# Memory's keys and values laid in other places, products on other banks, and the delta rule's late steps reordered

## What is computed

```python
h = rmsnorm(x, g_mix)
dq, dk, dv, dz, db, da, cq, ckv, kix, wix = split(h @ w_in)
dq, dk, dv = silu(causal_depthwise_conv([dq, dk, dv], conv_w))
g = -exp(a_log) * softplus(da + dt_bias)            # the gates: log decay per token and head
...
decay = exp(where(incl, g_cum[:, None] - g_cum[None, :], -inf))
a_mat = where(strict, beta * (k @ k.T) * decay, 0) + eye
sol = triangular_solve(a_mat, [v * beta, k * beta * exp(g_cum)])
for chunk in 4 chunks of 64 tokens:                 # gated delta rule, 4 heads
    v_new = u - w @ state; o = q_dec @ state + qk @ v_new; state = state * last + k_dec.T @ v_new
o_dn = rmsnorm(o) * silu(dz)
o_dsa = sparse_attention(cq, ckv, kix, wix)         # 8 heads, top 64 of 256 keys
x = x + concat(o_dn, o_dsa) @ w_out
kvx = rmsnorm(mem, g_mem) @ w_xkv                   # memory's keys and values, for cross attention behind this
```

## Time and profile before

| | us |
|---|---|
| median of 3 runs (lowest, highest) | 977.46 (975.92, 977.53) |
| the profiled execution | 976.31 |
| its span, first to last instruction | 974.5 |

### The profile page before, as it was taken

How to read it: one execution, slowest core, us unless ns; L and a number is a source line. 1 busy time by engine, 2 the same in 40 slices (tenths; PEclk the granted TensorE clock), 3 DMA queues, 4 the chain that set the end, 5 groups by cost and what they waited for, 6 DMA issues and landing times.

```text
span 974.5 us, 15544 instructions
## 1 busy us (share of the span) xinstructions
PE 950.0 (97%) x6212; PEld 848.5 (87%) x6212; DVE 679.7 (70%) x1247; ACT 530.4 (54%) x1011; POOL 125.6 (13%) x147
## 2 busy tenths in 40 slices
PE   8999999999999999999999799999899999999997
PEld 8999888999999988888988788988698898888885
DVE  5888767777478676666667659776665577676765
ACT  6876666765456643434455585664444354434443
POOL 1211111211032000000001115930100000000001
PEclk9999999999999999999999899999999999999999
DMA  9543334234377556565547534211353446656541
GB/s 317 186 140 131 130 105 155 94 124 132 129 252 239 173 181 216 173 215 171 194 152 262 164 108 133 105 44 44 132 172 130 151 138 207 201 170 199 171 168 43
DMA packets 116151, 154.71 MB, mean 159 GB/s; under 512 B 2760, under 2 KB 98256, under 8 KB 115824
## 3 DMA queue, kind: packets, MB, share of 16 engines
q1 hardware_dynamic: 113376, 142.91, 44.2%
q0 software_dynamic: 2240, 10.42, 3.1%
q10 hardware_dynamic: 464, 0.40, 0.2%
HBM read 150.56 MB, written 3.16 MB: 158 GB/s over the span
## 4 chain that ended last, share of the span: by engine, by line
PE 88%; DVE 6%; ACT 4%; issue 1%; DMA 1%; POOL 0%; POOLq 0%; DVEq 0%; SPq 0%; ACTq 0%
PE ps L827 13%; PE ps L803 9%; PE ps L805 8%; PE ps L804 8%; PE ps L828 7%; PE ps L1114 6%; PE ps L846 4%; PE ps L848 4%; PE ps L847 4%; PE ps L1087 4%; PE ps L1088 3%; PE ps L1089 3%; PE ps L789 3%; PE ps L816 2%; PE ps L818 2%; PE ps L817 2%
## 5 line engine op out<-in xcount | busy, mean ns | idle before, releaser
L1347 DVE TENSOR_TENSOR wlo<-raw,whi 128x1024 fp32r<-128x1024 f32 (+1 forms) x268 | 327.0, 1238 | 165.7 <-ACT whi L1958 165.4
L1958 ACT ACTIVATE whi<-raw 128x1024 fp32r<-128x1024 f32 (+1 forms) x268 | 274.4, 1051 | 138.3 <-PE ps L828 53.9
L827 PE MATMUL ps<-R1b,whi 128*128 128x512 f32 x576 | 201.8, 393 | 0.3 <-DVE wlo L1347 0.3
L803 PE MATMUL ps<-R1b,whi 128*128 128x256 f32 (+1 forms) x592 | 173.1, 292 | 5.5 <-DVE F L1635 3.0
L805 PE MATMUL ps<-R1b,wlo 128*128 128x256 f32 (+1 forms) x592 | 168.0, 284 | 0.0
L804 PE MATMUL ps<-R1b,whi 128*128 128x256 f32 (+1 forms) x592 | 167.8, 283 | 0.0
L828 PE MATMUL ps<-R1b,wlo 128*128 128x256 f32 x576 | 161.4, 280 | 0.0
L827 PEld LDWEIGHTS ps<-R1b,whi 128*128 128x128 f32 x576 | 108.1, 188 | 25.0 <-issue 0.8
L803 PEld LDWEIGHTS ps<-R1b,whi 128*128 128x128 f32 x592 | 112.0, 189 | 16.0 <-issue 8.6
L805 PEld LDWEIGHTS ps<-R1b,wlo 128*128 128x128 f32 x592 | 112.1, 189 | 0.0
L804 PEld LDWEIGHTS ps<-R1b,whi 128*128 128x128 f32 x592 | 111.8, 189 | 0.2
(11 more groups left out here) (279 smaller groups left out, 1786.6 us busy)
## 6 DMA issues: line engine op xcount, KB each, us to landing
raw<-in_w_in SPq DMA_DIRECT2D x34, 1024.0 KB, 5.1
raw<-in_w_ffn_in SPq DMA_DIRECT2D x22, 1024.0 KB, 5.1
raw<-in_w_ffn_out SPq DMA_DIRECT2D x11, 1024.0 KB, 5.5
raw<-in_w_gate SPq DMA_DIRECT2D x11, 1024.0 KB, 5.3
raw<-in_w_up SPq DMA_DIRECT2D x11, 1024.0 KB, 5.3
raw<-in_w_down SPq DMA_DIRECT2D x11, 1024.0 KB, 5.6
raw<-in_w_out SPq DMA_DIRECT2D x8, 1024.0 KB, 5.1
raw<-in_w_xkv SPq DMA_DIRECT2D x8, 1024.0 KB, 5.5
```

What stands on the lines that cost most here:

```text
L803: e.matmul(o, hi[:, kt, c], R[0][:, kt, 0:n], start=kt == 0, stop=False)
L827: e.matmul(B[:, :].rearrange("p (a n) -> p a n", a=2), hi[:, kt, c], R[2][:, :, kt, 0:256], start=kt == 0, stop=False)
L1347: e.tensor_tensor(half_of(wlo[i % HL], i, k), half_of(raw[i % RAW], i, k), f32(half_of(whi[i % HL], i, k)), SUB).then_inc(lo_split(i, (i, k)))
L1958: return e.activation(o, i, f, **kw)
```

## The change

Five groups of edits, which leave the arithmetic as it is:

- `tail` and the last values of the memory take banks of "four" and no longer of "big". `conv` 4 then finds banks 0 and 1 free since the transposes ahead of `tail`, and `conv` 8 takes bank 0 behind `conv` 6. In turn the memory's last values hold banks 5 and 6 from step 582 of the plan to 599: the sixteen `index` products, which before went round banks 7, 2, 4, 5, 3 and 6, go round 2, 3, 4 and 7, and `index` 0's fifth takes the bank of its first, `ssq` that of `index` 2's first, `kk` that of `index` 3's last.
- Keys lie in SC columns 1024 to 3071, the first values in 3072 to 4095, the last values in F, in Z's place. DT has its columns for itself; what waits for the store now is Xi and KD (`xi0`, `kn`) and, for the last values, Z (`zg`).
- `kvout` 0 moves from step 0 to 6, `kvout` 1 from ahead of `taps` 8 to behind it.
- `cums0`, `decay0`, `cums1` and `decay1` move a product later: `cums0` from behind `conv` 5 to behind `conv` 6, `cums1` and `decay1` (on ACT a table load, three small and eight large exponentials) from ahead of the split of unit 82 and `conv` 7 to behind them.
- At the end `rn_z` 0 and the split of unit 90's second half stand ahead of `chunk` 3, `rn_b` 0 ahead of `o1` 1, and `rn_z` 1 ahead of head 7's division.

```diff
-MIX = [(0, -1, ("kvout", 0)), (12, -1, ("kvout", 1))]
+MIX = [(6, 1, ("kvout", 0)), (13, 1, ("kvout", 1))]
...
-    (4, -1, "gates0", 0), (4, 1, "gates1", 0), (5, -1, "gates2", 0), (5, 1, "cums0", 0), (6, -1, "decay0", 0),
-    (7, -1, "cums1", 0), (7, -1, "decay1", 0), (10, -1, "ssq", 1), (10, 1, "scale", 0), (11, -1, "kk", 0), (11, -1, "inv", 0),
+    (4, -1, "gates0", 0), (4, 1, "gates1", 0), (5, -1, "gates2", 0), (6, 1, "cums0", 0), (7, -1, "decay0", 0),
+    (7, 1, "cums1", 0), (7, 1, "decay1", 0), (10, -1, "ssq", 1), (10, 1, "scale", 0), (11, -1, "kk", 0), (11, -1, "inv", 0),
...
-    (29, 1, "rn_a", 0), (31, 1, "rn_z", 0), (32, -1, "rn_a", 1), (32, 1, "rn_b", 0), (33, 1, "rn_z", 1), (34, 1, "rn_b", 1))]
+    (29, 1, "rn_a", 0), (32, -1, "rn_a", 1), (34, 1, "rn_b", 1))]
...
-MIX += [(31, 1, ("delta", "o1", 1))]
+MIX += [(30, 1, ("delta", "rn_z", 0)), (30, 1, ("ahead",)), (31, 1, ("delta", "rn_b", 0)),
+        (31, 1, ("delta", "o1", 1)), (32, 1, ("delta", "rn_z", 1))]
...
-                    two("mem", (1, u), part, i, ("four", "big")[u], R3a, normed("nm"), lambda t: (mem_act, (1, u, t)))
+                    two("mem", (1, u), part, i, "four", R3a, normed("nm"), lambda t: (mem_act, (1, u, t)))
...
-                two("tail", u, part, i, "big", R1, normed("nx2"), lambda t: (tail_dve, t))
+                two("tail", u, part, i, "four", R1, normed("nx2"), lambda t: (tail_dve, t))
...
                 if name == "decay0":
-                    d.wait_ge(kx_out, 0)
```

More of the change, by code:

```diff
@@ L225, in ahead @@
     def ahead(n=2 * HL, taken=0):
-        step("ahead", len(halves) + n, len(halves) + taken)
+        step("ahead", len(halves) + (n or 2 * HL), len(halves) + taken)
     def take(i, j):
@@ L327, in spread @@
                 if (at, side) == (k, 1):
-                    step(*token)
+                    ahead(0) if token == ("ahead",) else step(*token)
         for work, _ in works:
@@ L632, in program @@
         xsm = [F[:, 6144:7168], F[:, 7168:8192]]
+        keys, values_ = SC[:, 1024:3072].rearrange("p (b n) -> p b n", b=8), (SC[:, 3072:4096], F[:, 6180:7204])
         KX = SC[:, 0:2048].rearrange("p (b n) -> p b n", b=8)
@@ L2101, in mem @@
                         for t in range(2):
-                            act(VX[:, t, 512 * u:512 * u + 512], ps("mem", (1, u), t)[:, :]).then_inc(mem_act((1, u, t)))
+                            act(values_[u][:, 512 * t:512 * t + 512], ps("mem", (1, u), t)[:, :]).then_inc(mem_act((1, u, t)))
                     else:
-                        act(KX[:, 2 * u:2 * u + 2, :], ps("mem", (0, u))[:, :].rearrange("p (b n) -> p b n", b=2)).then_inc(
+                        act(keys[:, 2 * u:2 * u + 2, :], ps("mem", (0, u))[:, :].rearrange("p (b n) -> p b n", b=2)).then_inc(
                             mem_act((0, u)))
@@ L2157, in zg @@
                     a.wait_ge(gemm, ("zg", u))
+                    a.wait_ge(kv_out, 0)
                     for t in range(2):
@@ L2192, in delta @@
                     a.wait_ge(delta_dve, "edc")
-                    a.wait_ge(kv_out, 0)
+                    a.wait_ge(kx_out, 0)
                     a.wait_ge(gemm, ("mem", (1, 1)))
@@ L2420, in kvout @@
                 if u == 0:
-                    e.dma_start(kept[:, 0:2048], SC[:, 0:2048]).then_inc(kx_out(0), 16)
-                    e.dma_start(kept_v[:, :, 0:512], VX[:, :, 0:512]).then_inc(kx_out(0), 16)
-                else:
-                    e.dma_start(kept_v[:, :, 512:1024], VX[:, :, 512:1024]).then_inc(kv_out(0), 16)
+                    e.dma_start(kept[:, 0:2048], SC[:, 1024:3072]).then_inc(kx_out(0), 16)
+                values_u = values_[u].rearrange("p (t n) -> p t n", t=2)
+                e.dma_start(kept_v[:, :, 512 * u:512 * u + 512], values_u).then_inc((kv_out if u else kx_out)(0), 16)
             def kvin():
```

## The result

The changed kernel takes **980.4 us** (median of 10 runs, 978.81 to 982.64), the kernel before 977.11 us in the runs beside it (10, 975.92 to 978.8). The ratio is 1.0039, 95% interval 1.0027 to 1.0051: slower by 0.4%. The forecast was 979.0 with a range from 974.8 to 982.0. The profiled execution took 979.16 us, span 977.4, 2.9 more than the span before.

What follows compares the result with a forecast made beforehand. PE, busy 97% of the span, was taken as the bound, so only its waits count. Start -0.3, middle +1.4 and end +0.5 gave +1.6, taken as +1.5: 979.0 us, range 974.8 to 982.0.

Steps and rivals of the forecast that it cites:

- What bounds the kernel: Whole span: PE is busy 97%, so another engine's wait counts only where PE waits; five gaps, 9.8 us, are at stake.
- A: Start of the 32 matmuls of pre2 and pre3 on PE; 562.46 before, forecast 559.3 at full clock, 562.2 with it lowered.
- The start: From conv 4 to A: 3.1 us earlier at full clock, 2.9 taken for the low clock; -0.3 us, ends -3.1 and +0.4.
- The middle: From A to conv 8: 3.1 us of new idle at index, ssq and kk, conv 8's 1.69 gone; +1.4 us, -1.7 to +3.1.
- The rule on ACT's queue: ACT at the split of unit 82: its queue doesn't pass a waiting instruction; with it the middle is +1.4, otherwise -1.0.
- slower rival: Split of unit 82 on ACT: DVE late through key selection, conv 8's 1.69 stays; 980.8, or 983 with a second low clock; chance 0.20.
- The end: Last chunk to out: the subtraction 2.7 later, out's second half at 697.75 instead of 697.29; +0.5 us, ends -1.6 and +2.7.
- The clock didn't stay full: Judges the rival that PE's clock stays full at the start: A 3.1 earlier, sum -1.2, 976.2 us; chance 0.12.
- the waits were taken over: Judges the rival that the waits at tail's and the memory's banks go and nothing replaces them: 4.7 less, 972.8; chance 0.12.
- "nothing": Rival for the whole kernel: gaps move but their sum stays, no measurable change, 977.5 us; chance 0.12.
- the stores cost nothing: kvout 0 and kvout 1 at their new places cost 0; if POOL's cover failed, 0.75 us.
- The sum: Whole kernel: -0.3, +1.4 and +0.5 make +1.6, taken as +1.5; 977.8 against the profiled execution, 979.0 as median.

Runs made afterwards that it cites:

- old end: Changed kernel with rn_z 0, rn_b 0, rn_z 1 and the end's split put back at their old places; 978.22 us, ratio 1.0021 to the kernel before.
- the second experiment: Changed kernel with cums0, decay0, cums1 and decay1 back at their old places, a product earlier; 978.26 us, ratio 1.0021 to the kernel before.
- the layout's: Kernel before with only the changed layout of keys and values and the two kvout places; 976.12 us, ratio 0.9993 to the kernel before.
- memory on "big": Changed kernel with the memory's last values back on a bank of big, tail still on four; 978.15 us, ratio 1.0014 to the kernel before.
- the gates at their old place: Changed kernel with the gates' sums and the decay back at their old places; 978.26 us, ratio 1.0021 to the kernel before.
- the decay first and the memory on "four": Changed kernel with the old end, cums0 and decay0 ahead of pre1's transposes, cums1 and decay1 at old places; 973.23 us, ratio 0.9969 to the kernel before.
- the decay first: Changed kernel with old end, memory's last values on big, cums0 and decay0 ahead of pre1's transposes, cums1 and decay1 at old places; 972.31 us, ratio 0.9952.
- tail on big: Changed kernel with tail back on a bank of big, all else changed; 980.57 us, ratio 1.0045 to the kernel before.
- tail alone: Kernel before with one edit, tail on banks of four; 977.33 us, ratio 1.0005 to the kernel before.
- two edits: Kernel before with tail on four, and cums0 and decay0 behind conv 6 ahead of pre1's transposes; 972.23 us, ratio 0.9955 to the kernel before.
- the kernel without the split: Decay ahead of the transposes, memory on big, changed end without its split of unit 90's second half; 972.31 us, ratio 0.9958 to the kernel before.

## Why the prediction was right, and where it was not

**What bounds the kernel** held: between 537 and 600 the time follows PE's waits and the stretches of the lower clock, and A earlier by 4.1 gave 4.1 at the end.

**The start.** Each step came as worked out: `conv` 4 at 537.64, `conv` 6 behind a wait of 0.58, the sums at 549.81, 2.66 ahead of the transposes (2.8 said), a low stretch of 6.8 us as before. But that began at 550.5, 0.9 later than before, where I had said 2 to 4. I charged the clock 2.9 us. It took 1.9, because the wait of 2.66 lay inside the low stretch, and the lower clock cost nothing while PE idled. So the term was -1.25 in this execution instead of -0.3. In the old end's profile, with the same start, the stretch began at 552.6 and the term was -0.34, as I had said; the size depends on where the clock falls. (The term's high end, given as +0.4, is by its own sum, 559.3 + 3.4 against 562.46, +0.2.)

**The middle.** The rule on ACT's queue decided the first wait. The copy came at A + 11.5 (said A + 11.35), the wait was 1.31 (said 1.1), and with the exponentials ahead of the split, in the second experiment, it is gone. The row of ACT shows it: the load at 562.96 stood behind a split that waited 5.55 us. The Trainium skill says that ScalarE takes its queue strictly in order (TensorE: Matmul & The Clock Gate, section on the array and engine queue depths), and here the trace agrees. `ssq` and `kk` came at 1.17 and 0.86 (said 1.3 and 0.6), and the gap at `conv` 8 went. That makes +1.7 where I said +1.4. The other 1.6 of the measured +3.3 are the second low stretch of the clock (4.54 us for the memory's product instead of 2.95). The forecast's sum had no term for it; it stood only as an aside to the slower rival ("with the clock down a second time in these waits another 2 to 3"). This is the step that failed: the clock behind the three new waits was put at nothing.

**How much the second stretch weighs** is a question of how often. In the five profiles with the memory's last values on "four" the clock fell between 574 and 584 each time. In the seven with them on "big", the kernel before among them, it did so once, in the layout's, at 578 with no wait close ahead. Where the wait at `index` stood alone (memory on "big"), all 11 runs kept a mean clock of 0.994 or more. A row of waits isn't needed either: with the gates at their old place, and with the decay first and the memory on "four", the 1.17 ahead of `ssq` was PE's only wait between A and the fall. So the changed bank bought the 1.69 us of `conv` 8 for 2.03 of waits at two places and the clock behind them: some 1.5 to 2.4 us in the changed kernel, 0.9 with the decay first (both in one session). The profiled execution of the changed kernel had 3.4 us of it. Its six runs at 0.990 or 0.991 lack another 0.003 of 977, 3 us, which is some 6 us more at half speed (an estimate from these two clocks); where those lie no profile of this kernel shows, and it stays open. Three profiles of others (tail on big, tail alone, two edits) have a low stretch of 3.4 us between 687 and 695, at the waits of the end, which is one place where it could be.

**The end.** The last chunk's subtraction came 2.8 later, counted from the earlier chunk's products (said 2.7), the gap at `o1` was 1.29 (said 1.4), the one inside `out` 0.71 (said 0.8), the start of `out` all but unmoved as said. The second half came 1.0 later instead of 0.5. The chain of waits goes through the copy for head 6 (695.49), its products on PE (696.09), two products of `out` and only then the transposes of `rn_b` 1. I had let `rn_z` 1 start 0.4 earlier and save what the late mean cost. At 695.96 it was, without the shift of 2.20, where it stood before, and the transposes behind it had to wait for PE's queue anyway.

**The rivals.** The clock didn't stay full, the waits were taken over, and "nothing" is excluded by the interval. The slower rival's mechanism, DVE late through its selection of the keys, did not show: the 1.69 at `conv` 8 was saved, and the next wait of PE for DVE, at 639.59, was 0.34 long as before. What took its number was the clock. That the stores cost nothing held for the changed kernel; in the kernels with the changed layout and the memory on "big" this wait near 637 grew to between 0.86 and 1.03 (0.58 and 0.59 in the two with `tail` moved and the old layout).

**The sum.** Against the profiled execution of before I said 977.8 and measured 979.16; for the median 979.0 and 980.4. Both are 1.4 short: -0.95 at the start, +1.6 and +0.3 in the middle, +0.1 behind it and +0.5 at the end give 1.5; that I took 1.5 for a sum of 1.6 adds 0.1, and the 0.3 behind 745 take off again. The forecast's side, a little slower, holds; its own range (to 980.5) just takes the time in. Some of that is luck: the start's miss hid over a third of the others, and I had given half of the chances to a difference too small to tell (up to 979.4) and 0.35 to a slower kernel, which it is.

## What to carry to other kernels

When a wait is taken away, ask which input is late next at that place, and put in the gap the work that has its inputs already. Here freeing a bank gave nothing by itself (1.0005), and freeing it and moving the decay's sixteen matmuls into the gap gave 0.45%; the move without the bank was not tried. Work that waits for nothing should stand ahead of a split that waits, on an engine that takes its queue in order. Where a kernel has short waits in a row, look at several executions: the waits set the shortest time, and what they do to the clock sets how often a run reaches it.

## What the runs showed of the hardware

- Within the program the clock's lower level (0.50) came in stretches of about 3.4, 6.8 and 10.2 us in these profiles. Around the same waits its start moved from one execution to another: 550.5 in the changed kernel, 552.6 with the old end. The gap of 3.02 at `conv` 4 left the clock at 1.00 in the trace of before and was followed by 3.4 us at 0.50 in two other kernels in which the same gap stood (tail on big, layout alone). One kernel alone, that with the gates at their old place, took 976.65 to 976.97 in six runs at a mean clock of 0.994 or 0.995, and 979.5 to 981.1 in six at 0.990 or 0.991. The kernel before, in one session, ran from 978.74 at 0.991 to 973.11 at 0.999.
- Four scalings of DVE took 1.78 us beside two element instructions of POOL (687.28, 687.69), and 1.13 alone (695.96); so again in the kernel without the split (1.79). The Trainium skill says that the two engines share their way into SBUF where an instruction of DVE has two inputs there (GPSIMD Engine Reference, section on the specifications); these rows agree. Those 0.65 us are part of the 2.8 by which the last chunk's subtraction came later; without the split PE hardly felt them (a gap of 0.16).
